# Dense weights of the product-key experts: indirect accumulating DMAs into device memory in place of one-hot matmuls

## The reference

```
q = (xc @ wq).reshape(128, 8, 2, 128)                      # 8 heads, two halves
s1 = einsum('chd,hnd->chn', q[:, :, 0], keys1)             # 128 keys per half
s2 = einsum('chd,hnd->chn', q[:, :, 1], keys2)
v1, i1 = top_k(s1, 16);  v2, i2 = top_k(s2, 16)
cand = v1[..., :, None] + v2[..., None, :]                 # 256 pairs per head
best, pos = top_k(cand, 16)
eidx = (i1 * 128 + i2)[pos]                                # 16 experts per head
g = softmax(best)
a = einsum('chkd,cd->chk', u_tab[eidx], xc)
wgt = gelu(a) * g
out = einsum('chk,chkd->cd', wgt, v_tab[eidx])
```

## Time and profile before

| | |
|---|---|
| median of 3 runs | 2695.13 us (2693.18 to 2697.59) |
| profiled execution, first to last instruction (span; the page gives no other time of it) | 2693.3 us |
| PE busy | 2439.7 us, 91% |
| DVE busy | 1723.2 us, 64% |
| ACT busy | 1029.1 us, 38% |
| POOL busy | 406.0 us, 15% |
| DMA, mean | 225 GB/s |
| dense u products start; dense v products start | 1388.9 us (with the query products before them); 2124.2 us |

### The profile page before, as it was taken

The page is one execution under the profiler, slowest core; times in us unless marked ns, Lnnn a source line. Parts: engine busy times, 40 slices in busy tenths (PEclk is TensorE's granted clock), DMA queues, the critical chain, the costliest instruction groups (busy, mean ns, idle before and its releaser), DMA issues.

```text
span 2693.3 us, 30969 instructions
## 1 busy us (share of the span) xinstructions
PE 2439.7 (91%) x12205; PEld 1864.6 (69%) x12205; DVE 1723.2 (64%) x2984; ACT 1029.1 (38%) x1289; POOL 406.0 (15%) x299
## 2 busy tenths in 40 slices
PE   6888999578777899999989999989999999999996
PEld 4665786333333344677768999989999978777775
DVE  4535344421116657566543998899998578988886
ACT  4744532221004411477232343335655333333333
POOL 0100000000000000000000011132443234454430
PEclk9999999699987999999999999999999999999998
DMA  4454341599990100211022466779999799999992
GB/s 197 169 198 188 125 156 65 192 415 425 425 396 29 63 31 0 94 63 63 32 110 81 157 233 224 255 241 343 343 345 342 278 370 365 382 382 381 380 369 88
DMA packets 159278, 605.96 MB, mean 225 GB/s; under 512 B 13623, under 2 KB 79351, under 8 KB 126488
## 3 DMA queue, kind: packets, MB, share of 16 engines
q1 hardware_dynamic: 91168, 384.32, 37.9%
q0 software_dynamic: 42480, 154.68, 15.4%
q10 hardware_dynamic: 25480, 64.92, 6.2%
HBM read 533.10 MB, written 70.78 MB: 224 GB/s over the span
## 4 chain that ended last, share of the span: by engine, by line
PE 49%; DVE 24%; issue 11%; DMA 9%; ACT 5%; POOL 1%; ACTq 0%; DVEq 0%; SPq 0%; POOLq 0%
DVE window L597 6%; PE P L2590 4%; PE P L2592 4%; PE P L2591 4%; DVE part L597 4%; PE P L2245 3%; PE P L2421 3%; DVE ug L1397 3%; DMA H<-in_w_up 2%; DVE tmp L605 2%; DMA ug<-in_v,sparse 2%; PE P L2041 2%; PE P L2042 2%; PE P L2043 2%; DVE arena L597 1%
## 5 line engine op out<-in xcount | busy, mean ns | idle before, releaser
L597 DVE TENSOR_TENSOR part<-raw,part 128x2048 fp32r<-128x2048 f32 x136 | 311.1, 2288 | 164.2 <-ACT part L1896 162.6
L2590 PE MATMUL P<-hr,part 128*128 128x384 f32 (+1 forms) x1136 | 397.4, 350 | 17.1 <-DVE part L597 16.5
L2592 PE MATMUL P<-hr,part 128*128 128x384 f32 (+1 forms) x1136 | 391.5, 345 | 0.0
L2591 PE MATMUL P<-hr,part 128*128 128x384 f32 (+1 forms) x1136 | 391.3, 344 | 0.0
L2709 POOL DMA_INDIRECT ug<-in_ur,sparse x128 | 179.2, 1400 | 1213.7 <-DVE window L1289 751.2
L2694 PE MATMUL P<-part,ge 128*128 128x512 f32 x768 | 301.9, 393 | 13.3 <-DVE part L597 12.5
L2695 PE MATMUL P<-part,ge 128*128 128x512 f32 x768 | 299.0, 389 | 0.0
L2696 PE MATMUL P<-part,ge 128*128 128x512 f32 x768 | 299.0, 389 | 0.0
L1896 ACT ACTIVATE part<-raw 128x2048 fp32r<-128x2048 f32 x136 | 260.4, 1915 | 99.9 <-PE P L2696 80.8
L2590 PEld LDWEIGHTS P<-hr,part 128*128 128x128 f32 x1136 | 214.6, 189 | 27.9 <-DVE part L597 22.1
L2591 PEld LDWEIGHTS P<-hr,part 128*128 128x128 f32 x1136 | 214.7, 189 | 4.9
(11 more groups left out here) (363 smaller groups left out, 4419.8 us busy)
## 6 DMA issues: line engine op xcount, KB each, us to landing
raw<-in_u SPq DMA_DIRECT2D x64, 1024.0 KB
raw<-in_vd SPq DMA_DIRECT2D x64, 1024.0 KB
W<-in_w_up SPq DMA_DIRECT2D x24, 2048.0 KB, 18.8
W<-in_w_in SPq DMA_DIRECT2D x18, 2048.0 KB, 8.0
W<-in_ada_w SPq DMA_DIRECT2D x12, 2048.0 KB, 7.8
a_scratch<-gt ACTq DMA_DIRECT2D x128, 192.0 KB
w_scratch<-window ACTq DMA_DIRECT2D x12, 2048.0 KB, 11.7
wr<-w_scratch SPq DMA_DIRECT2D x32, 768.0 KB, 13.0
```

Of the source, the lines that this page charges most:

```text
L597: return v.tensor_tensor(out=out_, in0=in0, in1=in1, op=op)
L2590: t.matmul(b, wh[:, k, js], HR[0][:, k, lo:S], start=k == 0, stop=False)
L2591: t.matmul(b, wh[:, k, js], HR[1][:, k, lo:S], start=False, stop=False)
L2592: ins = t.matmul(b, wl[:, k, js], HR[0][:, k, lo:S], start=False, stop=k == 7)
```

## The change

`Wd` becomes a flat array with one element per expert and token. It is zeroed by 12 DMAs of 2 MB on POOL after the attention of the first block. `places` replaces `columns`: for block q it writes the flat element number (expert x 384 + token) of each of the 128 pairs of 128 tokens, and `shares` writes their shares to `WGT`. POOL then adds one column (one pair of each of 128 tokens, 4 bytes each) per indirect DMA with `compute_op=ADD`: 3 blocks x 128 columns = 384 of them, in 24 rounds of 16 (a round is one head, whose 16 experts differ; `add_weights(q, h)` waits until the round before it of the same block has landed). POOL gets its own list `POOL_STEPS`: four rows of u, a round, four rows of u, and so on. All of the one-hot work of DVE, PE and ACT and the three transposes go; the load of W in `chunk` reads rows of 1536 bytes instead of 512.

```diff
-        behind = {1: "ex", 4: "sm", 8: "tx", 12: "gt"}
+        behind = {1: "ex", 4: "sm", 8: "of"}
...
-        wg_steps = interleave([("wg", x, i) for x in range(48) for i in range(2)], dots, 0.75) + dots
         last = [ahead.pop() for _ in range(10)][::-1]
-        ORDER3 += interleave(wg_steps, ahead, len(ahead) / len(wg_steps))
+        ORDER3 += interleave(dots, ahead, len(ahead) / len(dots))
...
+        ROUNDS = [(1, h) for h in range(4)] + [x for h in range(4) for x in ((2, h), (1, h + 4))]
+        ROUNDS += [x for h in range(4) for x in ((3, h), (2, h + 4))] + [(3, h) for h in range(4, 8)]
+        POOL_STEPS, rounds, ready = [("row", k) for k in range(4)], list(ROUNDS), set()
+        for kind, *i in ORDER3:
+            if kind == "of":
+                ready.add(i[0])
+            if kind == "ud" and i[0] % 4 == 0:
+                POOL_STEPS += [("row", k) for k in range(i[0] + 4, i[0] + 8)]
+                if rounds and rounds[0][0] in ready:
+                    POOL_STEPS.append(("add", *rounds.pop(0)))
+        POOL_STEPS += [("add", *x) for x in rounds]
...
+            def places(q):
+                num = EQ[:, 0:1, 0:8, :].rearrange("p h k j -> p (h k j)")
+                tk_wait()
+                tk_inc(stt(num, hk2(I1), 128.0, hk2(I2), MUL, ADD))
+                tk_wait()
                 if q == 0:
...
+                    tk_inc(v.tensor_copy(EID, num), ("of", 0))
+                else:
+                    tk_inc(stt(num, num, float(DN), par("slot", q - 1).broadcast_to([128, 128]), MUL, ADD))
...
-            def weights(x, n):
-                o2, oa, ob, oc = OB[x % 2]
...
-                    tt(two(o2), every, rows(I2T), EQ_).then_inc(s["wg_v"], 1)
-                    tt(two(O1), every, rows(I1T), EQ_).then_inc(s["wg_v"], 1)
-                else:
-                    dve.wait_ge(s["wg_v"], at + 2)
-                    for i, y in enumerate((oa, ob, oc)):
-                        tt(two(y), two(O1), rows(GT[i]), MUL).then_inc(s["wg_v"], 1)
...
+            zeros = reg(44, 1)
+            gp.wait_ge(s["att_mm"], 68)
+            g.memset(zeros, 0.0).then_inc(s["wz_v"], 1)
+            gp.wait_ge(s["wz_v"], 1)
+            for i in range(12):
+                nc.gpsimd.dma_start(Wd.rearrange("(p r x) o -> p r (x o)", p=128, x=S)[:, 8 * i:8 * i + 8, :],
+                                    zeros.unsqueeze(1).broadcast_to([128, 8, S])).then_inc(s["wz"], 16)
...
+            def add_weights(q, h):
+                gp.wait_ge(s["wz"], 192)
+                gp.wait_ge(s["tk_v"], mark["of", q])
+                gp.wait_ge(s[f"st{q}"], 256 * h)
+                for k in range(16 * h, 16 * h + 16):
+                    g.indirect_dma_start(out=Wd, out_offset=bass.IndirectOffsetOnAxis(ap=OFS[q - 1][:, k:k + 1], axis=0),
+                                         in_=WGT[q - 1][:, k:k + 1], in_offset=None, compute_op=ADD).then_inc(s[f"st{q}"], 16)
...
-                nc.sync.dma_start(WRB[n % 2].rearrange("p (b i) -> p b i", b=12),
-                                  Wd.rearrange("b p (c i) -> c p b i", c=32)[n]).then_inc(s[f"wq{n % 2}"], 16)
+                nc.sync.dma_start(k4(WRB[n % 2]), Wd.rearrange("(c i p t) o -> c p i (t o)", i=4, p=128, t=DN)[n]).then_inc(s[f"wq{n % 2}"], 16)
...
                 elif kind == "spill":
-                    sp.wait_ge(s["ws0"], 96)
-                    sp.wait_ge(s["ws1"], 96)
-                    sp.wait_ge(s["wg_v"], 241)
-                    sp.wait_ge(s["wg_mm"], 96)
+                    for q in (1, 2, 3):
+                        sp.wait_ge(s[f"st{q}"], 2048)
                     chunk(0)
```

More of the change, by code:

```diff
@@ L506, in program @@
         GS, GR = SMALL[:, 1920:1928], SMALL[:, 1928:1936]
-        TOK = wreg(28, 4).bitcast(bf16)
-        I1T, I2T, *GT = [TOK[:, 2 * DN * i:2 * DN * i + 2 * DN].rearrange("p (t e) -> p t e", e=2) for i in range(5)]
+        TOK = wreg(28, 4)
+        OFS = [TOK[:, 128 * q:128 * q + 128].bitcast(u32) for q in range(3)]
+        WGT = [TOK[:, 384 + 128 * q:512 + 128 * q] for q in range(3)]
         iota16 = iota[:, 0:16].unsqueeze(1).broadcast_to([128, 128, 16])
[L511 to L515, removed]
         window.close()
@@ L555, in program @@
         sums = [("sv", k) for k in range(128)]
-        known = best.index(("gt", 0)) + 6
+        known = best.index(("of", 0)) + 6
         best = best[:known] + interleave(best[known:], dots, 0.6)
@@ L578, in program @@
         assert not sums
[L580 to L586, removed]
+        ROUNDS = [(1, h) for h in range(4)] + [x for h in range(4) for x in ((2, h), (1, h + 4))]
[9 more added lines that the diff above has]
+        POOL_STEPS += [("add", *x) for x in rounds]
+        n_rows = sum(x[0] == "row" for x in POOL_STEPS)
         GM = (1, 2, 4, 6)
-        ta_of = lambda q: 1 + 3 * q
         mark = {}
@@ L1412, in row_sum @@
                     stt(YT[0], VG[(k + 4) % 8], DOT[:, k:k + 1], YT[0], MUL, ADD).then_inc(s["ys_v"], 1)
-            def weights(x, n):
-                o2, oa, ob, oc = OB[x % 2]
[L1416 to L1427, removed]
-                    tt(two(o2), every, rows(I2T), EQ_).then_inc(s["wg_v"], 1)
-                    tt(two(O1), every, rows(I1T), EQ_).then_inc(s["wg_v"], 1)
-                else:
-                    dve.wait_ge(s["wg_v"], at + 2)
-                    for i, y in enumerate((oa, ob, oc)):
-                        tt(two(y), two(O1), rows(GT[i]), MUL).then_inc(s["wg_v"], 1)
             def weighted(n):
-                ww = WRB[n % 2].rearrange("p (b i t) -> p i b t", b=12, i=4)
-                dve.wait_ge(s["wg_mm"], 96)
+                ww = k4(WRB[n % 2])
+                dve.wait_ge(s["sc_mm"], 16)
                 dve.wait_ge(s[f"gin{n % 2}"], 16 * (n // 2 + 1))
@@ L1448, in weighted @@
                         tt(GE[n % 2][1][:, i - 1, :], GIN[n % 2][:, i - 1, :], GE[n % 2][0][:, i - 1, :].bitcast(f32), SUB).then_inc(s["gm_v"], 1)
-            for kind, *i in ORDER3V:
+            for kind, *i in ORDER3:
                 if kind == "tk":
@@ L1454, in vector_program @@
                     shares(*i)
-                elif kind == "gt":
-                    columns(*i)
-                elif kind == "wg":
-                    weights(*i)
+                elif kind == "of":
+                    places(*i)
                 elif kind == "fx" and i[2] == 1:
@@ L2756, in row_of_v @@
                     if k % 8 < 4:
-                        gp.wait_ge(s["wg_v"], 241)
-                        gp.wait_ge(s["wg_mm"], 96)
+                        for q in (1, 2, 3):
+                            gp.wait_ge(s[f"st{q}"], 2048)
                     rows(VG[(k + 4) % 8], A["v"], EID[:, k:k + 1], s[f"vg{k % 4}"])
-            for kind, *i in ORDER3 + V_STEPS:
-                if kind == "ud":
-                    for k in range(4) if i[0] == 0 else (i[0] + 3,):
-                        row_of_u(k)
+            for kind, *i in POOL_STEPS:
+                if kind == "row":
+                    row_of_u(*i)
+                else:
+                    add_weights(*i)
+            for kind, *i in V_STEPS:
+                if kind == "ud" and n_rows <= i[0] + 3 < 128:
+                    row_of_u(i[0] + 3)
                 elif kind in ("vr", "sw"):
@@ L2982, in layout @@
     p["odd"] = np.broadcast_to(np.arange(32) % 2, (128, 32))
+    p["slot"] = np.arange(128)[:, None] + 128 * np.arange(3)
     p["row0"] = np.broadcast_to(np.cumsum([0] + [16 // (i + 1) for i in range(15)]), (128, 16))
```

106 lines of the change are left out of this document (14 added, 92 removed), and 1 row of the table s.

## The result

The changed kernel takes 3173.72 us (median of 4 runs, 3168.25 to 3176.98) against 2696.36 (2693.18 to 2699.39) for the kernel before, measured with it: a ratio of 1.177, 95% interval 1.1755 to 1.1784. It is 477 us slower. The forecast was 2977 with a range of 2790 to 3290.

The account below looks back on a forecast made before the run. PE and DVE were taken as full in the one-hot stretch, with only POOL having room; POOL's additions would then delay v by 282 us: 2693.3 + 282 - 8 + 3 + 5 = 2975, median 2977, range 2790 to 3290.

Parts of the forecast that it names:

- The payload is not POOL's work, so I take the same 1.24.: POOL's 384 additions: each priced like a gather, 0.94 us plus 0.30 gap; chance of this forecast 0.52.
- an addition costs POOL more than a gather: Rival on POOL's issue price: up to 2.18 us per addition with gap; 3157 us half way, 3338 at the end; chance 0.36.
- POOL beside DVE: Contention of POOL's issues with DVE until the last addition: 23 plus 74, together 97 us, bounds 0 and 278.
- 472 issues: POOL's stretch from the first round: 384 additions and 88 rows at 1.24 us, 585 us at least.
- First round at 1679: Start of POOL's additions: after the 20th row, done at 1689.4 in the earlier trace, less 10 us for earlier places.
- Landing 9.1 us: SP's wait after the last addition for it to land: 9.1 us, as the gathers of h rows take.
- 35.8 to the first v product: From the first load of W to the first v product: 35.8 us, the same order of loads as before.
- the +5 for PE's clock behind the wait: Last two u units and first v products behind SP's wait: low PE clock costs 0 to +17 us, taken as +5.
- The DMA term of 0: DMA engines during the additions: 4-byte transfers cost next to nothing, taken as 0; upper bound 504 us of each engine.
- PE idles some 250 us: Stretch of additions before the v stage: PE waits for low parts and idles some 250 us.
- PE's 83 us: u stage: removing the small one-hot matmuls frees 83 us of PE, so v would start 83 us sooner if POOL kept up.
- The equal point: Price of an addition, gap and contention included, at which the time equals that before: 0.71 us; chance of equal 0.01.

Follow-up runs that it names:

- the version with one-hot work: Against the kernel before: the first of three blocks added by 128 accumulating DMAs, the other two keep their one-hot matmuls; 2770.14 us, ratio 1.027.
- the two versions without additions: Changed kernel with its 384 additions left out, 2623.37 us; version with only block one by additions, its 128 additions left out, 2669.40 us.

## Why the prediction was right in sign and range, and short by 197 us

**The mechanism was right.** POOL without a free microsecond from 1687 to 2570, DVE waiting for rows, PE for low parts, then SP's wait, and an unchanged v stage. All of this is in the views after. (One sign could not come: POOL "90% busy". The gaps are not counted as busy, so 0.94 in 1.24 is 76%; it was 83%, with the gaps 100%.) Half or none of the additions, additions made cheaper, and gathers ahead of all of them moved the time by what they do to POOL's sum.

**The term that was mis-sized: "The payload is not POOL's work, so I take the same 1.24."** The prediction said that it is wrong if the mean addition is above 1.6; it is 1.70. With nothing running beside it an addition takes 1.55, against 0.94: (1.55 - 0.94) x 384 = 234 us, more than the whole miss of 197. That the sum missed by less is luck: the contention term was too large (next paragraph) and gave 35 back. The case that the forecast put second, "an addition costs POOL more than a gather", is what happened: half way between its bounds stood 1.71 with the gap and 3157 us; the measured 1.55 + 0.30 = 1.85 lies inside them, two thirds of the way. Its reason ("two reads per write") isn't shown, only that accumulating costs 0.58. The nearest row was a gather, and a gather is another operation; with ends at 1.24 and 2.18 and no row on accumulation, the chances of 0.52 and 0.36 leaned too far on it. The range held only because it included most of that second case.

**"POOL beside DVE", 97 us, was too much.** The additions' stretch is 384 x (1.700 - 1.546) = 59 us, and that of the 88 gathers some 3 us. Most of them lie behind 1800 us, where they take 0.965 in the mean:

```profile
L2611 POOL DMA_INDIRECT ug<-in_ur,sparse x76 | 73.3, 965 | 23.2 <-issue 23.2
```

Together 62. As additions slow the dots, DVE is emptier than the share of 0.28 that I scaled by (9 of 50 us at 1900). The run without accumulation, with the same DVE work in less time, has more of it for each DMA (0.20), the run with half of the additions 0.29, and the version with one-hot work 0.42. So the price per issue rises with how full DVE is, and falls when more issues share the same DVE work.

**472 issues.** Forecast for POOL's stretch 585 + 97 = 682 us, measured 1687.44 to 2570.04 = 882.6. The difference of 201 is 234 - 35 and 1.8 of a landing wait.

**First round at 1679.** It came at 1687.44, 8 us later:

```profile
1684.39 2.75 POOL L2611 DMA_INDIRECT ug<-in_ur,sparse  x1 [8.89 <-DVE ug L1383]
1687.44 2.69 POOL L2663 DMA_INDIRECT w_scratch<-window  x1 [0.30 <-issue]
```

The 20th row is done at 1687.1, 2.3 us before that of the earlier trace rows, though the u stage began 7.5 us later (1396.37). So the step's 10 us for the earlier places held (9.8), and what it missed is the late start.

**Landing 9.1 us.** It was 1.5: the last issue ends at 2570.04 and SP's load follows at 2571.56. The h rows' 9.1 of the earlier trace rows is a median from issue to landing of 4 KB rows. From the start of its issue the last addition took 3.1, so the row was the wrong one for 4 bytes. **35.8 to the first v product** was 33.8, at a granted clock of 0.60 from 2550 to 2600, so the +5 for PE's clock behind the wait was not there. Together: 2406 + 8 + 201 - 8 - 2 = 2605, where v starts.

**The small terms.** The zeroing's issues were put at 12 x 8 x 0.547 = 52 us; POOL needs 0.89 for each DMA of 1024 rows, 10.6 in all: eight times the rows took 1.6 times as long, and not eight times. "In a stretch where DMA is little used" was wrong for 350 to 400 us, where the share was 0.54 before and 1.02 after. The time of 0 to +15 held (3.6 us for the zeroing alone; the u stage starts 7.5 later). The v stage gained 1.5 us and not 8: larger pieces of W did not help PE, which idles 31.3 us for low parts where it idled 34.4. The DMA term of 0 was right, since the share is 0.46 to 0.57 from 1800 to 2500; the 504 us bound was far off. PE's clock, 0.60 to 0.77 there, is hidden, as said, because PE waits anyway. "PE idles some 250 us" did not follow from the sum, which has v 282 us later and 83 us of work gone, thus 365; it idled 516 for low parts between 1687 and 2605.

**The two rules.** "GPSIMD Engine Reference" of the Trainium skill ("Key points") has the contention with VectorE, and the runs agree, from 0.01 us more for an addition beside an idle DVE to 0.42 beside one busy 38 of 50 us. By the fit of 2.0 us per DMA in "DMA: Bandwidth & Descriptors" of the Trainium skill ("Anatomy of one DMA — SWDGE (gpsimd) path"), taken without overlap, the time would have been 3269 by the prediction's estimate. That is nearer than my sum, but for a reason that the trace does not bear out: an addition has landed some 3.1 us after its issue began (the last one), and issues begin 1.85 apart, so they overlap, and 1.55 of the 1.85 is POOL's time to issue.

**The gain that was there.** PE's 83 us was 73 in the run without additions, which includes the zeroing and the 7 us later start. Its first load of W came the full 83 us sooner (2005.48 against 2088.34); behind it the first v product took 46 us in place of 35.8. The equal point, 0.71 us for an addition with its gap and contention, lies far below the 1.70 + 0.30 = 2.00 that one costs.

## What to carry to other kernels

Moving work from a full engine to an idle one pays only as far as the idle one's queue has waits to give. Count its idle microseconds in the stretch (here 188 and 233 in the two versions without additions), multiply the new instructions by their own price and compare, before anything about bytes. Here the price of an accumulating indirect DMA was one of issuing: paid mostly per instruction, little per place, and 0.58 us above that of a plain one. When only a related operation is in the trace, its duration is a guess for the one that does more, and the forecast should lean to the dearer side.

## What the runs showed of the hardware

- An accumulating indirect DMA of 128 places holds POOL for 1.55 us, one of 64 for 1.41, a plain scatter of 128 for 0.96, a gather of 128 rows for 0.94; each with a gap of 0.30 behind it.
- A direct DMA of 1024 rows holds POOL for 0.89 us, one of 128 rows for 0.55.
- What DVE's work beside them adds does not go with the number of additions: 59 us in all with 384, 56 with 192, 54 with 128 beside two thirds of the one-hot work, 78 with 384 plain scatters, and 4 (384 x 0.01) with nothing beside them. What it does go with isn't shown: the version with one-hot work has many more DVE operations and no more of it.
- 49,152 updates of 4 bytes don't fill the DMA engines: with nothing else running their share is 0.22.
- PE, busy 11 to 19 of 50 us in the two windows shown, was granted 0.60 to 0.68, and 1.00 again in the v stage, where it is busy 49.
